# Small gaps between the tiles of a feed-forward: the same instructions at other addresses

## The chip, the cores and the metric

The kernel runs on one core of one Trainium2 chip. The metric is the time of one execution on the device, in microseconds. The engines are named TensorE (PE in the profile, PEld for its weight loads), VectorE (DVE), ScalarE (ACT), GpSimd (POOL) and SyncE (SP, which issues the DMAs here). Tiles lie in SBUF, which has 128 partitions; the address of a tile is a number of bytes within each partition. Sums of matmuls are kept in PSUM.

## What is computed

One decoder layer on a sequence of 2048 rows of 1024 numbers, in float32. The change touches the last part, the feed-forward:

```python
def reference(x, ...):
    h = rms_norm(x, g_pre_mix[l])
    proj = h @ w_in[l]
    ...                       # retention and dilated attention, joined to mix
    mix = jnp.concatenate([ret, att], axis=-1) @ w_out[l]
    x = x + rms_norm(mix, g_post_mix[l])
    h = rms_norm(x, g_pre_ffn[l])
    f = (jax.nn.silu(h @ w_gate[l]) * (h @ w_up[l])) @ w_down[l]
    x = x + rms_norm(f, g_post_ffn[l])
```

w_gate and w_up are 1024 x 2816, w_down is 2816 x 1024.

## The kernel before

The program runs five phases one after another: a norm with transposes, the input projection (L376 is its matmul), attention, the mixer with the output projection (L1034), and the feed-forward `ffn`. Each phase allocates its own tiles; when a phase ends, their room is given to the next.

**Matmuls.** Every large product is made of three: a float32 operand is split into a high part and a low part (`_hi`, `_lo`, type float32r), and hi x hi, hi x lo and lo x hi are summed in PSUM. Each matmul has a stationary tile of 128 x 128, loaded first by a weight load (LDWEIGHTS), and a moving tile of 128 x 512 that streams past it. In a call `matmul(out, a, b)` a is the stationary one and b the moving one.

**The feed-forward** takes the sequence in two halves of 1024 rows, each half as two groups (UG) of 512, and the 2816 inner columns in 11 parts (J) of 256, which are two tiles of 128. For each half, part and group:

- gate and up (L1415): for each of two tiles and for gate and up, 8 steps over the 1024 inputs, 3 products each: 24 matmuls. Stationary is a block of 128 columns of `w_hi` or `w_lo`, moving is `h_hi` or `h_lo`. The sum goes to `gu_ps`.
- ScalarE takes the silu into `gated` (L1473), VectorE multiplies by up (L1541), ScalarE copies to `a_hi` (L1475), and VectorE subtracts to `a_lo` (L1543).
- down (L1433): for each of four chunks of 128 rows and two halves of 512 output columns, 2 tiles with 3 products. Stationary is a block of `a_hi` or `a_lo`, moving is `down_hi` or `down_lo`. The sum goes to `d_ps`, and VectorE adds it to `total` (L1556, L1553).

TensorE's own order is gate_up(J, 0), down(J-1, 1), gate_up(J, 1), down(J, 0). The weights of part J+1 are loaded to `raw` and `down_raw` by SyncE while part J is computed; ScalarE makes their high parts and VectorE their low parts (L1459, L1528, L1466, L1534). At the end of each half the rows of `total` are normed (`ssq`, `squares`, `gain`), added to `x1` and stored (L1569, L1572, L1359).

**Where the tiles lie.** They are placed one after another, in the order in which they are declared, from one fixed base on; each takes a multiple of 32 bytes. Counted from that base, the tiles of the feed-forward begin at these bytes: h_hi 0, h_lo 32768, total 65536, raw 98304, w_hi 114688, w_lo 131072, down_raw 147456, down_hi 155648, down_lo 163840, gated 172032, a_hi 176128, a_lo 184320, gain 192512, x1 196608, squares 204800. All are multiples of 4096.

The input projection has hT_hi at 0 and hT_lo at 65536 (moving), `w_hi` at 135168 and `w_lo` at 143360 (stationary). The output projection of the mixer, L1034, has `w_hi` at 32768 and `w_lo` at 65536 (moving), and mT_hi at 184672 and mT_lo at 192864 (stationary). Its chain is the same three products over 8 steps:

```python
for k in range(KT):
    for a, w in ((mT_hi, w_hi), (mT_hi, w_lo), (mT_lo, w_hi)):
        last = nc.tensor.matmul(y_ps[:, half, :], a[:, s, k, :], w[:, k, half * GROUP:(half + 1) * GROUP],
```

Of the kernel before, what the change touches and what calls it, by code (L numbers as in the profile page):

```python
# [14 lines left out]
P = 128  # L15
# [1258 lines left out]
def ffn(nc, D):  # L1274
# [11 lines left out]
    with ExitStack() as ctx:  # L1286
        m = Mem(nc, ctx, "ff")
        h_hi = m.sb("h_hi", [P, KT, HALF], F32R)
        h_lo = m.sb("h_lo", [P, KT, HALF], F32R)
        total = m.sb("total", [P, UG * UC, DM])  # L1290
        raw = m.sb("raw", [P, 2, KT, PW])
        w_hi = m.sb("w_hi", [P, 2, KT, PW], F32R)
        w_lo = m.sb("w_lo", [P, 2, KT, PW], F32R)
        down_raw = m.sb("down_raw", [P, TILES, DM])
        down_hi = m.sb("down_hi", [P, TILES, DM], F32R)
        down_lo = m.sb("down_lo", [P, TILES, DM], F32R)
        gated = m.sb("gated", [P, TILES, GROUP])
        a_hi = m.sb("a_hi", [P, UG, TILES, GROUP], F32R)
        a_lo = m.sb("a_lo", [P, UG, TILES, GROUP], F32R)
        gain = m.sb("gain", [P, DM])  # L1300
        x1 = m.sb("x1", [P, 2, DM])
# [339 lines left out]
def build(nc, aps):  # L1641
    D = tensors(nc, aps)
    with ExitStack() as ctx:
        keep = {n: ctx.enter_context(nc.sbuf_tensor(n, [P, KT, SEQ], F32R)) for n in ("hT_hi", "hT_lo")}
        keep["w_raw"] = ctx.enter_context(nc.sbuf_tensor("w_raw", [P, KT, P], F32))
        spent = normed_transpose(nc, D, keep)
        project(nc, D, keep)
    with ExitStack() as ctx:
        w_out = ctx.enter_context(nc.sbuf_tensor("w_out", [P, KT, DM], F32))
        attention(nc, D, w_out, spent)  # L1650
        mix(nc, D, w_out)
    ffn(nc, D)
# [48 lines left out]
```

## Time and profile before

| | |
|---|---|
| median of the runs, us | 2872.72 (2870.31 to 2874.89) |
| profiled execution, us | 2876.43 |
| its span, first to last instruction, us | 2874.6 |
| TensorE busy | 93% of the span |
| VectorE, ScalarE, GpSimd busy | 43%, 25%, 22% |
| mean granted clock of TensorE | 0.966 |
| span moved by DMA | 269.6 MB, 94 GB/s |

TensorE's clock has two levels in the profile, 2.4 GHz (granted clock 1.00) and 1.2 GHz (0.50). The busy time that the profile gives for one matmul is longer than the distance from its start to the start of the next, since matmuls overlap. What a matmul costs in a stream of them is that distance. It is read from the starts in the timeline, or from the chain of waits, where a row gives the time that so many matmuls took together.

### The profile page before, as it was taken

Reading aid. Unit: us, or ns where it says so; the run is one execution under the profiler, and the core shown is the slowest. Engines: PE = TensorE matmul, PEld = TensorE weight load, DVE = VectorE, ACT = ScalarE, POOL = GpSimd, SP = SyncE. Lnnn points to the kernel's source line nnn. Section 1 sums busy time; section 2 is a strip of 40 time slices with the busy share of each in tenths; the row PEclk is TensorE's granted clock in tenths of the full one; section 3 lists DMA queues with packets and bytes.
Section 4 is the critical chain, followed back from the end, with each engine's and each line's share of the span. In section 5 each row is a group of like instructions: output and inputs, shape, how many; then the busy total and the mean of one; then the engine's idle time right before and its main releaser. Section 6 shows DMA issues by size and latency. Waiting matters only on the chain.

```text
span 2874.6 us, 36337 instructions
## 1 busy us (share of the span) xinstructions
PE 2663.6 (93%) x13096; PEld 2230.9 (78%) x13096; DVE 1227.9 (43%) x2271; ACT 723.0 (25%) x1402; POOL 626.8 (22%) x403
## 2 busy tenths in 40 slices
PE   6999999968989979998599999999999999999995
PEld 4777777758989857776488888888888888888884
DVE  6102455305555568886233333333354333333334
ACT  4112111116666622222111111111121111111111
POOL 2952544204443167674000000000010000000000
PEclk9999999989999979999799999999999999999998
DMA  4222223343446145654711112111253111211103
GB/s 173 70 66 66 66 102 109 117 119 106 115 123 184 50 139 170 191 169 140 263 44 45 44 44 72 45 44 44 103 179 99 44 44 44 68 49 44 44 15 102
DMA packets 220445, 269.62 MB, mean 94 GB/s; under 512 B 12224, under 2 KB 164672, under 8 KB 220096
## 3 DMA queue, kind: packets, MB, share of 16 engines
q1 hardware_dynamic: 220352, 268.42, 29.5%
q8 instruction: 53, 0.87, 0.1%
q14 instruction: 40, 0.33, 0.0%
HBM read 188.29 MB, written 80.08 MB: 93 GB/s over the span
## 4 chain that ended last, share of the span: by engine, by line
PE 49%; DMA 2%; DVE 1%; SPq 0%; issue 0%; ACT 0%; POOL 0%; DVEq 0%; ACTq 0%
PE ff_psum_gu L1415 33%; PE ff_psum_down L1433 16%; DMA out<-ff_x 1%; DMA ff_h_lo<-h_lo 0%; DMA ff_x<-x 0%; SPq L1348 0%; DVE ff_x L1572 0%; DVE ff_total L1569 0%; DVE ff_total L1556 0%; DVE ff_down_lo L1534 0%; DVE ff_w_lo L1528 0%; SPq L1353 0%; SPq L1337 0%; DVE ff_gated L1541 0%; DVE ff_total L1553 0%
## 5 line engine op out<-in xcount | busy, mean ns | idle before, releaser
L1415 PE MATMUL ff_psum_gu<-ff_h_hi,ff_w_hi 128*128 128x512 f32 x1408 | 549.6, 390 | 22.1 <-DMA ff_h_lo<-h_lo 22.1
L1415 PE MATMUL ff_psum_gu<-ff_h_lo,ff_w_hi 128*128 128x512 f32 x1408 | 549.1, 390 | 0.0
L1415 PE MATMUL ff_psum_gu<-ff_h_hi,ff_w_lo 128*128 128x512 f32 x1408 | 548.9, 390 | 0.0
L1520 POOL TENSOR_TENSOR ff_ssq<-ff_ssq,ff_minus_half 128x1 f32<-128x1 f32 x16 | 14.4, 906 | 1466.4 <-DVE ff_ssq L1561 1466.4
L1541 DVE TENSOR_TENSOR ff_gated<-ff_gated,ff_psum_gu 128x512 f32<-128x512 f32 x88 | 60.5, 687 | 628.7 <-PE ff_psum_gu L1415 628.7
L376 PE MATMUL pr_psum_acc<-hT_hi,pr_w_hi 128*128 128x512 f32 x768 | 304.1, 396 | 24.4 <-DVE pr_w_lo L315 14.2
L1415 PEld LDWEIGHTS ff_psum_gu<-ff_h_hi,ff_w_hi 128*128 128x128 f32 x1408 | 265.2, 188 | 77.9 <-issue 18.5
L1415 PEld LDWEIGHTS ff_psum_gu<-ff_h_lo,ff_w_hi 128*128 128x128 f32 x1408 | 265.3, 188 | 55.2
L1415 PEld LDWEIGHTS ff_psum_gu<-ff_h_hi,ff_w_lo 128*128 128x128 f32 x1408 | 265.1, 188 | 55.3
L376 PE MATMUL pr_psum_acc<-hT_lo,pr_w_hi 128*128 128x512 f32 x768 | 301.1, 392 | 0.0
L376 PE MATMUL pr_psum_acc<-hT_hi,pr_w_lo 128*128 128x512 f32 x768 | 301.1, 392 | 0.0
L1433 PE MATMUL ff_psum_down<-ff_down_hi,ff_a_hi 128*128 128x512 f32 x704 | 274.8, 390 | 14.9 <-DVE ff_total L1556 13.9
L1556 DVE TENSOR_TENSOR ff_total<-ff_total,ff_psum_down 128x1024 f32<-128x1024 f32 x160 | 195.2, 1221 | 202.4 <-PE ff_psum_down L1433 202.4
L1433 PE MATMUL ff_psum_down<-ff_down_hi,ff_a_lo 128*128 128x512 f32 x704 | 274.4, 390 | 0.0
L1433 PE MATMUL ff_psum_down<-ff_down_lo,ff_a_hi 128*128 128x512 f32 x704 | 274.4, 390 | 0.0
L376 PEld LDWEIGHTS pr_psum_acc<-hT_hi,pr_w_hi 128*128 128x128 f32 x768 | 145.6, 190 | 64.2 <-issue 24.4
L1475 ACT ACTIVATE ff_a_hi<-ff_gated 128x512 fp32r<-128x512 f32 x88 | 55.6, 632 | 498.9 <-DVE ff_gated L1541 498.9
L650 PE MATMUL at_psum_o<-at_vblk,at_probT 128*128 128x65 f32 x1200 | 162.8, 274 | 10.6 <-ACT at_probT L755 7.5
L1473 ACT ACTIVATE ff_gated<-ff_psum_gu 128x512 f32<-128x512 f32 x88 | 52.6, 598 | 476.0 <-PE ff_psum_gu L1415 476.0
L376 PEld LDWEIGHTS pr_psum_acc<-hT_hi,pr_w_lo 128*128 128x128 f32 x768 | 145.5, 189 | 30.9
L376 PEld LDWEIGHTS pr_psum_acc<-hT_lo,pr_w_hi 128*128 128x128 f32 x768 | 145.8, 190 | 29.7
L766 ACT ACTIVATE at_prob<-at_prob,at_orow 128x256 f32<-128x256 f32 (+1 forms) x384 | 155.2, 454 | 54.3 <-DVE at_orow L710 53.3
(158 smaller groups left out, 3979.0 us busy)
## 6 DMA issues: line engine op xcount, KB each, us to landing
ff_raw<-in_w_gate SPq DMA_DIRECT2D x22, 1024.0 KB, 5.3
ff_raw<-in_w_up SPq DMA_DIRECT2D x22, 1024.0 KB, 7.8
ff_down_raw<-in_w_down SPq DMA_DIRECT2D x22, 1024.0 KB, 4.7
projT<-pr_rows SPq DMA_DIRECT2D x64, 256.0 KB, 2.4
att_out<-at_orow SPq DMA_DIRECT2D x192, 66.0 KB, 1.8
mx_att_in<-att_out SPq DMA_DIRECT2D x16, 792.0 KB, 4.8
w_raw<-in_w_in SPq DMA_DIRECT2D x24, 512.0 KB, 4.3
nt_xin<-in_x SPq DMA_DIRECT2D x16, 512.0 KB, 3.4
```

The costliest lines, as they stand in the source:

```text
L376: last = nc.tensor.matmul(acc[:, s, g, :], w[:, s, k, :], h[:, k, t], start=n == 0, stop=n == 3 * KT - 1)
L650: last = nc.tensor.matmul(o_ps[:, j % 2, h, 0:OW], probT[:, j % 2, h, kb, :], vblk[:, j - 1 + kb, h, :], start=kb == first, stop=kb == 1)
L766: last = nc.scalar.activation(pr, pr, ACT.Exp, bias=orow[:, j % RING, 2 * OW + h:2 * OW + h + 1], scale=-1.0)
L1415: last = nc.tensor.matmul(gu_ps[:, tile, n], w[:, n, k, cols], h[:, k, t], start=i == 0, stop=i == 3 * KT - 1)
L1433: last = nc.tensor.matmul(d_ps[:, c % 2, half * GROUP:(half + 1) * GROUP], a[:, g, tile, c * P:(c + 1) * P], w[:, tile, half * GROUP:(half ...
L1473: nc.scalar.activation(gated[:, tile], gu_ps[:, tile, 0], ACT.Silu).then_inc(silu_done, 1)
L1475: nc.scalar.activation(a_hi[:, g, tile], gated[:, tile], ACT.Copy).then_inc(a_hi_done, 1)
L1520: nc.gpsimd.tensor_tensor(ssq[:, c], ssq[:, c], minus_half[:], ALU.pow).then_inc(rooted, 1)
L1541: nc.vector.tensor_tensor(gated[:, tile], gated[:, tile], gu_ps[:, tile, 1], ALU.mult).then_inc(mul_done, 1)
L1556: nc.vector.tensor_tensor(to, to, d_ps[:, c % 2], ALU.add).then_inc(added, 1)
```

## The change

Five gap tiles are declared between the tiles of the feed-forward: of 64, 64, 256, 128 and 32 bytes in each partition. Nothing reads or writes them. Every instruction is the same as before and in the same order on its engine; only the addresses in it differ. Lines behind the change are numbered 5 higher (L1415 becomes L1420, L1433 becomes L1438).

```diff
         total = m.sb("total", [P, UG * UC, DM])
         raw = m.sb("raw", [P, 2, KT, PW])
+        m.sb("gap0", [P, 16])
         w_hi = m.sb("w_hi", [P, 2, KT, PW], F32R)
+        m.sb("gap1", [P, 16])
         w_lo = m.sb("w_lo", [P, 2, KT, PW], F32R)
+        m.sb("gap2", [P, 64])
         down_raw = m.sb("down_raw", [P, TILES, DM])
         down_hi = m.sb("down_hi", [P, TILES, DM], F32R)
         down_lo = m.sb("down_lo", [P, TILES, DM], F32R)
         gated = m.sb("gated", [P, TILES, GROUP])
+        m.sb("gap3", [P, 32])
         a_hi = m.sb("a_hi", [P, UG, TILES, GROUP], F32R)
+        m.sb("gap4", [P, 8])
         a_lo = m.sb("a_lo", [P, UG, TILES, GROUP], F32R)
```

## Rows read from the trace of the kernel before

**Rows 1.** Page, part 1: engine, busy us, share of the span, instructions

```profile
PE 2663.6 (93%) x13096; PEld 2230.9 (78%) x13096; DVE 1227.9 (43%) x2271; ACT 723.0 (25%) x1402; POOL 626.8 (22%) x403
```

**Rows 2.** Timeline, TensorE, feed-forward's first matmuls: start us, us, engine, line, out<-in

```profile
1396.71 0.76 PE L1415 MATMUL ff_psum_gu<-ff_h_hi,ff_w_hi 128*128 128x512 f32 x1 [18.12 <-DMA ff_h_lo<-h_lo]
...
1397.70 0.63 PE L1415 MATMUL ff_psum_gu<-ff_h_hi,ff_w_lo 128*128 128x512 f32 x1
...
1398.98 0.63 PE L1415 MATMUL ff_psum_gu<-ff_h_hi,ff_w_lo 128*128 128x512 f32 x1
```

**Rows 3.** Timeline, all engines, the end of the program

```profile
2857.53 0.39 PE L1433 MATMUL ff_psum_down<-ff_down_hi,ff_a_lo 128*128 128x512 f32 x1
2859.24 1.22 DVE L1572 TENSOR_TENSOR ff_x<-ff_x,ff_total 128x1024 f32<-128x1024 f32 x1 [0.79 <-DMA ff_x<-x]
...
2866.72 1.28 DVE L1569 SCALAR_TENSOR_TENSOR ff_total<-ff_total,ff_ssq,ff_gain 128x1024 f32<-128x1024 f32 x1 [0.66 <-POOL ff_ssq L1520]
```

**Rows 4.** Stretches: from:to, length, busy us by engine, granted clock, DMA share, GB/s

```profile
core 0: us, PE busy (x) PEld busy (x) DVE busy (x) ACT busy (x) POOL busy (x), PEclk, DMA share, GB/s
1397.00:1399.00 2.00, 2.00 (x6) 1.52 (x6) 0.00 (x0) 0.00 (x0) 0.00 (x0) 0.50 1.11 353
1450.00:2180.00 730.00, 728.99 (x3217) 603.30 (x3216) 269.18 (x272) 128.67 (x172) 8.15 (x8) 1.00 0.21 71
```

**Rows 5.** Waits after 1400 us, TensorE's: us in total, times, longest

```profile
PE ff_psum_down L1433 <- DVE ff_total L1556: 13.9, 1, 13.9
...
PE ff_psum_gu L1415 <- DMA ff_h_lo<-h_lo: 4.0, 1, 4.0
...
PE ff_psum_down L1433 <- DVE ff_total L1553: 1.0, 1, 1.0
```

**Rows 6.** Chain of waits in order of time: start us, us, what

```profile
1491.94 21.76 PE ff_psum_gu L1415 x96
1513.70 10.88 PE ff_psum_down L1433 x48
...
2309.24 21.76 PE ff_psum_gu L1415 x96
```

**Rows 7.** Page, part 5: group, count, busy us, mean ns, idle before

```profile
L1415 PE MATMUL ff_psum_gu<-ff_h_lo,ff_w_hi 128*128 128x512 f32 x1408 | 549.1, 390 | 0.0
...
L1433 PE MATMUL ff_psum_down<-ff_down_hi,ff_a_lo 128*128 128x512 f32 x704 | 274.4, 390 | 0.0
```

**Rows 8.** Timeline, TensorE's matmuls, in the feed-forward

```profile
1499.94 0.39 PE L1415 MATMUL ff_psum_gu<-ff_h_hi,ff_w_hi 128*128 128x512 f32 x1
1500.16 0.39 PE L1415 MATMUL ff_psum_gu<-ff_h_lo,ff_w_hi 128*128 128x512 f32 x1
```

**Rows 9.** Timeline, TensorE's weight loads, the same moment

```profile
1499.94 0.19 PEld L1415 LDWEIGHTS ff_psum_gu<-ff_h_lo,ff_w_hi 128*128 128x128 f32 x1
1500.17 0.19 PEld L1415 LDWEIGHTS ff_psum_gu<-ff_h_hi,ff_w_lo 128*128 128x128 f32 x1
```

**Rows 10.** Timeline, TensorE, output projection: thirteen starts, first and last

```profile
1351.00 0.39 PE L1034 MATMUL mx_psum_y<-mx_w_hi,mx_mT_lo 128*128 128x512 f32 x1
...
1353.81 0.39 PE L1034 MATMUL mx_psum_y<-mx_w_hi,mx_mT_lo 128*128 128x512 f32 x1
```

**Rows 11.** Stretches in the output projection and early in the feed-forward, columns as above

```profile
1412.00:1416.00 4.00, 4.00 (x19) 3.34 (x18) 0.11 (x1) 0.00 (x0) 0.00 (x0) 1.00 1.05 386
1351.00:1353.90 2.90, 2.90 (x14) 2.25 (x12) 0.00 (x0) 0.00 (x0) 0.00 (x0) 1.00 0.76 231
```

**Rows 12.** Timeline, TensorE, early feed-forward: sixteen starts, first and last

```profile
1412.22 0.39 PE L1415 MATMUL ff_psum_gu<-ff_h_hi,ff_w_hi 128*128 128x512 f32 x1
...
1415.62 0.39 PE L1415 MATMUL ff_psum_gu<-ff_h_hi,ff_w_hi 128*128 128x512 f32 x1
```

**Rows 13.** Timeline, TensorE, behind a wait of the down matmuls: seven starts, then two more

```profile
2173.28 0.39 PE L1433 MATMUL ff_psum_down<-ff_down_lo,ff_a_hi 128*128 128x512 f32 x1
...
2174.67 0.39 PE L1433 MATMUL ff_psum_down<-ff_down_lo,ff_a_hi 128*128 128x512 f32 x1
2174.90 0.39 PE L1433 MATMUL ff_psum_down<-ff_down_hi,ff_a_lo 128*128 128x512 f32 x1
2175.12 0.39 PE L1433 MATMUL ff_psum_down<-ff_down_hi,ff_a_hi 128*128 128x512 f32 x1
```

## The prediction

> **What bounds the kernel now.** I read the share line of TensorE and the granted clock first, then the stretches of the feed-forward, then what TensorE waits for in it, then the chain of waits, and last the starts of single matmuls.
>
> The page says that TensorE is busy for 93% of the span, and VectorE for 43% [rows 1]. The feed-forward begins with its first matmul at 1396.71 us [rows 2] and ends with its last at 2857.53 us [rows 3]. Between 1450 and 2180 us TensorE is busy for 728.99 of 730 us at a granted clock of 1.00, which is the 2.4 GHz level, and VectorE and ScalarE are busy for 269 and 129 us [rows 4]. After 1400 us TensorE's idle time is 13.9 + 4.0 + 1.0 us, three waits in 1460 us [rows 5]. So this half of the program is one stream of matmuls, and nothing else can set its time but the distance from one matmul's start to the next.
>
> The busy time of one matmul (390 ns) is no such distance, since matmuls overlap. The chain of waits gives it: 96 gate and up matmuls take 21.76 us, 48 down matmuls take 10.88 us, both 226.7 ns each, and such rows alternate through the whole stage [rows 6]. The feed-forward has 2 x 11 x 2 x 2 x 2 x 24 = 4224 gate and up matmuls and 2 x 11 x 2 x 4 x 2 x 12 = 2112 down matmuls, 6336 in all (the page's counts are 3 x 1408 and 3 x 704 [rows 7]). 6336 x 226.7 ns = 1436 us of the 1460.8 us of the stage: **one nanosecond more or less per matmul is 6.3 us of the whole**.
>
> At the 1.2 GHz level the same matmuls start 427 ns apart: three distances from 1397.70 to 1398.98 us [rows 2]. The granted clock there is 0.50 [rows 4]. That is 512 columns at 1.2 GHz (426.7 ns) with nothing on top. At 2.4 GHz the columns alone would be 213.3 ns, but the rows show 226.7. So 13.3 ns of each matmul, 84 us of the program, is something that the slow clock hides, and the only other thing that TensorE does at that moment is to read the next stationary tile: while the matmul of 1499.94 us runs, the load for the next one starts, at 1499.94 us too, and takes 0.19 us [rows 8, 9].
>
> **Does an address matter at all?** The change alters nothing but base addresses, so I looked for two places in this trace that do the same thing at different ones. Write every base as a distance in bytes from the first tile of its phase. In the feed-forward before, all bases are multiples of 4096. The input projection's tiles (hT_hi 0, hT_lo 65536, w_hi 135168, w_lo 143360) are multiples of 4096 too. The output projection of the mixer (L1034) has its moving tiles at multiples of 4096, but its stationary tiles mT_hi and mT_lo at 184672 and 192864, 352 bytes past one. 352 is an odd multiple of 32, every other distance is a multiple of 64.
>
> Its matmuls have the same shape and type, and the same order of three products as the down matmuls. Yet twelve distances from 1351.00 to 1353.81 us take 2.81 us, **234.2 ns each and not 226.7** [rows 10]. Other engines are not the reason: in that stretch VectorE, ScalarE and GpSimd are busy for 0.00 us, at a granted clock of 1.00 [rows 11]. The DMA engines are not either: they are at 0.76 there, while between 1412 and 1416 us they are at 1.05 [rows 11] and fifteen gate and up distances from 1412.22 to 1415.62 us are 226.7 ns each all the same [rows 12]. What is left as the difference is the address of the stationary tile: 7.5 ns a matmul.
>
> A third thing shows in the feed-forward itself: after a wait the distance is not 226.7 at once. From 2173.28 us the next six distances are 1.39 us together, **231.7 ns each**, before it settles at 226.7 or so (2174.67, 2174.90, 2175.12) [rows 13]. So 226.7 is a rhythm that the matmuls fall into, and while anything keeps disturbing it the mean is some 5 ns higher.
>
> **The change, part by part.** No instruction is added, removed or reordered; the gap tiles are never touched. Bases after, as distances from h_hi: w_hi 114752 (+64), w_lo 131200 (+128), down_raw, down_hi, down_lo and gated +384, a_hi +512, a_lo +544, gain, x1 and squares +544. h_hi, h_lo, total and raw stay, as does everything before the feed-forward: 0 us there.
>
> - Gate and up, 4224 matmuls: moving h stays, the stationary tiles shift by 64 and 128 bytes and remain multiples of 64. No row shows such a shift alone. Bounds: 0, or what the mixer's address shows, 7.5 x 4224 = +31.7 us; below nothing, the whole excess, -13.3 x 4224 = -56.2 us. The strides within w_hi and w_lo give the nearest evidence: column blocks 512 bytes apart run at one distance, so shifts of 512 and its multiples do nothing. Whether 64 and 128 do is not shown; I take **0**, since the one slow place differs by an odd multiple of 32, which these shifts are not.
> - Down, 2112 matmuls: moving down_hi and down_lo shift by 384, the stationary a_hi by 512 (nothing by the above), a_lo by 544, an odd multiple of 32 like mT's 352. One weight load in three, 704, gets the mixer's kind of address. Low: only these pay, 704 x 7.5 = +5.3 us. High: the rhythm is lost for all three products, 2112 x 7.5 = +15.8 us. Between them is the case that one disturbed load in three never lets it settle, the price of [rows 13]: 2112 x 5.0 = **+10.6 us**. I take this, as the settling takes six matmuls and the disturbance returns every third.
> - VectorE and ScalarE operands, and the weight transfers: hidden, because VectorE is busy for 269 of 730 us and TensorE waits for no transfer there. If an operation took twice its time they would still fit.
> - The end: from 2857.53 us the last rows of the output go through gain, x1 and squares, shifted by 544, 17.1 us with no cover. Its VectorE operations are 1.2 to 1.3 us each [rows 3]. I take 0, at most 1 us either way.
>
> Sum: 0 + 10.6 + 0 + 0 = +10.6 us. The profiled execution's own time is 2876.4 us with a span of 2874.6; it lies 3.7 us above the median of 2872.7. Against its own time the changed kernel would be 2887; against the median, which I forecast, **2872.7 + 10.6 = 2883.3 us**, and 2878 to 2889 by the two bounds of the down term.
>
> The rows show each load under the matmul before it [rows 8, 9]. The Trainium skill, in TensorE: Matmul & The Clock Gate, Step-by-step, says that loading the next tile's weights "doesn't steal SBUF read bandwidth from the running matmul", and SBUF — State Buffer, under the two separate sides, that PE never waits on anyone. By that rule no address could matter, and the time would be that before; the 234.2 beside 226.7 ns speaks against it, but does not prove the address. The first of these pages also gives 215.7 ns for 512 columns back to back; the rows show 226.7, so whatever the 11 ns between them are, it is a cost that some arrangement may not have.
>
> **The rivals.**
> - *No difference.* The mixer's pace has another cause (its PSUM tile, the operations around it), or a_lo's shift costs under 2 ns a load. For it: the feed-forward keeps one distance for three pairs of tiles with bases tens of kilobytes apart. Against it: beyond its address and its PSUM tile nothing in [rows 10] differs from the down matmuls. That the gaps don't move the tiles at all belongs here; since sizes are whole multiples of 32 bytes they do. Time: 2872.7, within 3.
> - *Slower all over.* What counts is that moving and stationary bases are congruent modulo 128 or more, which before holds for every fast place and after for none. Its place is the gate and up stage as well: it decides as soon as the shift of 64 costs over 1.4 ns. Gate and up alone, 2872.7 + 31.7 = 2904; with down, 6336 x 7.5 = +47.5, 2920 us.
> - *Faster.* Both streams start on the same multiple, so that each weight read meets the matmul's reads in the same part of the memory; moving one by 64 bytes takes it out of the way. Its ceiling is 13.3 x 6336 = 84 us, 2788 us; half of it 2830. For it: the excess is there, and absent at the slow clock. Against it: a weight load sweeps 512 bytes while the matmul sweeps 2048, so a shift under 512 moves where they meet, not how often; and no settled distance under 226.7 stands anywhere in the trace.
>
> **How the numbers follow.** Forecast 0.35, no difference 0.25, slower all over 0.21, faster 0.19. The likeliest gives 2883. Its low end is about the 0.2% (5.7 us) that a measurement can tell from no change, so 0.03 of it counts as same: faster 0.19, same 0.28, slower 0.53. The range must take in no difference and slower all over (2920), and may leave out most of faster: 2862 to 2922, which leaves out about 0.18 below and 0.02 above; signs are mixed, and the forecast's own range stands above.
>
> **What would show it.** In the profile after, the chain's rows for 48 down matmuls would read 11.0 to 11.3 instead of 10.88, and those for 96 gate and up matmuls 21.76. Gate and up rows at 22.1 or more mean slower all over; 21.5 or less, faster. The mixer must be unchanged. A down row of 10.88 makes the reading of the mixer wrong; a time that moved with both rows unchanged makes all of it wrong.

## The result: 1.2% slower

| | before | changed |
|---|---|---|
| median, us | 2873.46 (2870.31 to 2874.89) | 2909.22 (2905.06 to 2910.40) |
| ratio, 95% interval | | 1.0123 (1.0106 to 1.0141) |
| profiled span, us | 2874.6 | 2908.6 |
| granted clock, mean | 0.966 | 0.963 |

The changed kernel takes 35.8 us more, where +10.6 was forecast. In the profile after, the chain of waits in order of time (start us, us, what) reads:

```profile
1517.97 11.20 PE ff_psum_down L1438 x48
1529.17 22.19 PE ff_psum_gu L1420 x96
...
2331.26 22.19 PE ff_psum_gu L1420 x96
2353.44 11.20 PE ff_psum_down L1438 x48
```

These answer to [rows 6]. 96 gate and up matmuls take 22.19 us instead of 21.76, which is 231.1 ns from start to start instead of 226.7. 48 down matmuls take 11.20 us instead of 10.88, 233.3 ns each. There are 44 blocks of each kind, so the rows give 44 x 0.43 + 44 x 0.32 = 18.9 + 14.1 = **33.0 us** of a span that grew by 34.0 us.

Nothing else moved. These are the waits of TensorE after 1400 us (us in total, times, longest):

```profile
PE ff_psum_gu L1420 <- DMA ff_h_lo<-h_lo: 21.1, 2, 18.3
PE ff_psum_down L1438 <- DVE ff_total L1561: 13.8, 1, 13.8
PE ff_psum_down L1438 <- DVE ff_total L1558: 0.5, 1, 0.5
```

And this is the stretch of [rows 4] again, with its columns:

```profile
core 0: us, PE busy (x) PEld busy (x) DVE busy (x) ACT busy (x) POOL busy (x), PEclk, DMA share, GB/s
1450.00:2180.00 730.00, 730.00 (x3151) 591.44 (x3150) 256.83 (x259) 123.92 (x166) 8.14 (x8) 1.00 0.20 67
```

The first row holds the feed-forward's first wait of 18.3 us, which in the kernel before (18.12 us) ended just ahead of 1400 us [rows 2]; without it 2.8 us are left where [rows 5] has 4.0. So the idle time is that of before, the clock is 1.00 as before, and VectorE and ScalarE do the same work at a slower rate. TensorE has 3151 matmuls in 730 us, where it had 3217. The same instructions each start later. Starts of single matmuls, fifteen distances apart:

```profile
1599.93 0.40 PE L1420 MATMUL ff_psum_gu<-ff_h_hi,ff_w_hi 128*128 128x512 f32 x1
...
1603.40 0.40 PE L1420 MATMUL ff_psum_gu<-ff_h_hi,ff_w_hi 128*128 128x512 f32 x1
```

3.47 us / 15 = 231.3 ns, against the 226.7 of [rows 12].

### The profile page after: what moved, and what is told of

The parts are those of the page before. It is cut to its first block, busy times and chain, and to the rows that moved or that the text cites. A ratio compares the mean times of both kernels' runs of the same rounds, so it can differ in the third digit from the quotient of the medians.

```text
span 2908.6 us, 36337 instructions
## 1 busy us (share of the span) xinstructions
PE 2692.2 (93%) x13096; PEld 2228.2 (77%) x13096; DVE 1228.9 (42%) x2271; ACT 722.7 (25%) x1402; POOL 630.4 (22%) x403
## 4 chain that ended last, share of the span: by engine, by line
PE 49%; DMA 2%; DVE 1%; SPq 0%; issue 0%; ACT 0%; POOL 0%; DVEq 0%; ACTq 0%
PE ff_psum_gu L1420 33%; PE ff_psum_down L1438 17%; DMA out<-ff_x 1%; DMA ff_x<-x 0%; DMA ff_h_lo<-h_lo 0%; SPq L1353 0%; DVE ff_x L1577 0%; DVE ff_total L1561 0%; DVE ff_total L1574 0%; DVE ff_down_lo L1539 0%; DVE ff_w_lo L1533 0%; POOL ff_ssq L1525 0%; SPq L1342 0%; DVE ff_gated L1546 0%; DVE ff_total L1558 0%
## 5 line engine op out<-in xcount | busy, mean ns | idle before, releaser
L1420 PE MATMUL ff_psum_gu<-ff_h_hi,ff_w_hi 128*128 128x512 f32 x1408 | 561.9, 399 | 21.1 <-DMA ff_h_lo<-h_lo 21.1
L1420 PE MATMUL ff_psum_gu<-ff_h_hi,ff_w_lo 128*128 128x512 f32 x1408 | 553.7, 393 | 0.0
L1420 PE MATMUL ff_psum_gu<-ff_h_lo,ff_w_hi 128*128 128x512 f32 x1408 | 550.8, 391 | 0.0
L1420 PEld LDWEIGHTS ff_psum_gu<-ff_h_hi,ff_w_hi 128*128 128x128 f32 x1408 | 265.3, 188 | 79.7 <-issue 18.6
L1420 PEld LDWEIGHTS ff_psum_gu<-ff_h_hi,ff_w_lo 128*128 128x128 f32 x1408 | 265.6, 189 | 67.3
L1420 PEld LDWEIGHTS ff_psum_gu<-ff_h_lo,ff_w_hi 128*128 128x128 f32 x1408 | 265.7, 189 | 58.7
L1438 PE MATMUL ff_psum_down<-ff_down_hi,ff_a_hi 128*128 128x512 f32 x704 | 277.4, 394 | 14.3 <-DVE ff_total L1561 13.8
L1438 PE MATMUL ff_psum_down<-ff_down_lo,ff_a_hi 128*128 128x512 f32 x704 | 281.5, 400 | 0.0
L1438 PE MATMUL ff_psum_down<-ff_down_hi,ff_a_lo 128*128 128x512 f32 x704 | 278.5, 396 | 0.0
L1438 PEld LDWEIGHTS ff_psum_down<-ff_down_hi,ff_a_hi 128*128 128x128 f32 x704 | 132.8, 189 | 49.1 <-DVE ff_total L1561 14.2
```

The source lines that it names most:

```text
L1420: last = nc.tensor.matmul(gu_ps[:, tile, n], w[:, n, k, cols], h[:, k, t], start=i == 0, stop=i == 3 * KT - 1)
L1438: last = nc.tensor.matmul(d_ps[:, c % 2, half * GROUP:(half + 1) * GROUP], a[:, g, tile, c * P:(c + 1) * P], w[:, tile, half * GROUP:(half ...
```

## The experiments

### Only the shifts of gate and up

```diff
         raw = m.sb("raw", [P, 2, KT, PW])
+        m.sb("gap0", [P, 16])
         w_hi = m.sb("w_hi", [P, 2, KT, PW], F32R)
+        m.sb("gap1", [P, 16])
         w_lo = m.sb("w_lo", [P, 2, KT, PW], F32R)
+        m.sb("gap2", [P, 96])
         down_raw = m.sb("down_raw", [P, TILES, DM])
```

> Only the stationary tiles of gate and up are shifted as in the change (w_hi +64, w_lo +128 bytes against h); down's tiles are shifted by 512 together. Theory A (the distance from matmul to matmul is set by where its own stationary and moving tiles lie, modulo 512): 96 gate and up matmuls take 22.19 us as in the changed kernel, 48 down matmuls 10.88 us as before; 4224 x 4.5 ns = +19 us over before. Rival B (the slower pace comes from the addresses that VectorE, ScalarE or the transfers use, or from the down tiles): gate and up stay at 21.76 us and the time at +0. Rival C (large shifts like 512 matter too): down leaves 10.88.

Measured: 2893.82 against 2873.77 us, ratio 1.0066 (1.0051 to 1.0082), +20.0 us. The first matmuls of one gate and up block, of the down block behind it, and of the next block, in the timeline of TensorE:

```profile
1722.63 0.40 PE L1418 MATMUL ff_psum_gu<-ff_h_hi,ff_w_hi 128*128 128x512 f32 x1
...
1744.82 0.39 PE L1436 MATMUL ff_psum_down<-ff_down_hi,ff_a_hi 128*128 128x512 f32 x1
...
1755.70 0.40 PE L1418 MATMUL ff_psum_gu<-ff_h_hi,ff_w_hi 128*128 128x512 f32 x1
```

22.19 us for the 96, as in the changed kernel, and 10.88 us for the 48, as before. Theory A holds, but for its period, which this run leaves open: shifts of 64 and 128 bytes are enough, and down, whose tiles all lie 512 bytes further, is untouched. B and C fall as they are put. VectorE and ScalarE also write `w_hi` and `w_lo` at the shifted addresses here; that their writes are not what costs is shown only by the scan below, where no other engine works.

### Only the shifts of down

```diff
         w_lo = m.sb("w_lo", [P, 2, KT, PW], F32R)
+        m.sb("gap2", [P, 96])
         down_raw = m.sb("down_raw", [P, TILES, DM])
@@
+        m.sb("gap3", [P, 32])
         a_hi = m.sb("a_hi", [P, UG, TILES, GROUP], F32R)
+        m.sb("gap4", [P, 8])
         a_lo = m.sb("a_lo", [P, UG, TILES, GROUP], F32R)
```

> Only down_raw, down_hi, down_lo, gated (+384), a_hi (+512) and a_lo (+544) are shifted as in the change; gate and up lie as before. Theory A: gate and up 21.76 us for 96, down 11.20 us for 48 as in the changed kernel; 2112 x 6.7 ns = +14 us. Rival B: down stays at 10.88 us because the weights of gate and up disturb the whole stream.

Measured: 2885.61 us, ratio 1.0038 (1.0025 to 1.0051), +11.8 us. The chain of waits:

```profile
1514.94 11.19 PE ff_psum_down L1436 x48
1526.13 21.79 PE ff_psum_gu L1418 x96
```

Down runs as in the changed kernel, so B falls. Gate and up take 21.79 us, 0.03 more than before: in the trace the first five distances of a block are 228.4 to 235.8 ns in the mean of the blocks, and from the sixth on they are 226.7, much as in [rows 13]. The two halves, 20.0 and 11.8 us, make 31.8 of the 35.8; the rest is within the intervals of the three measurements. For this part the blocks give 44 x 0.31 + 44 x 0.03 = 15.0 us, and the runs 7 to 15, so the runs say less than the blocks of what down costs.

### The mixer's stationary tiles aligned

```diff
+        m.sb("gap0", [P, 40])
         mT_hi = m.sb("mT_hi", [P, 2, KT, P], F32R)
         mT_lo = m.sb("mT_lo", [P, 2, KT, P], F32R)
```

> Before, with one gap of 160 bytes ahead of mT_hi in the mixer, so that mT_hi and mT_lo lie at a multiple of 512 bytes from the moving tiles instead of 352 past a multiple of 4096. Theory A: the output projection's distance falls from 234.2 to 226.7 ns; 768 matmuls x 7.5 ns = 5.8 us at most, less where the mixer waits for VectorE: -2 to -5.8 us. Rival (the output projection is slower for its PSUM tile or its surroundings): 234.2 ns and the time stay.

Measured: 2872.85 us, ratio 0.9995 (0.9986 to 1.0004). The output projection (L1034 is L1035 here), twelve distances apart in the timeline:

```profile
1347.01 0.39 PE L1035 MATMUL mx_psum_y<-mx_w_hi,mx_mT_hi 128*128 128x512 f32 x1
...
1349.73 0.39 PE L1035 MATMUL mx_psum_y<-mx_w_hi,mx_mT_hi 128*128 128x512 f32 x1
```

2.72 us / 12 = 226.7 ns, where [rows 10] had 234.2 with the same PSUM tile and surroundings. So the reading of [rows 10] was right: it was the address. But little of the 5.8 us reaches the time: its interval is -4.0 to +1.1 us, which holds nothing as well as the upper part of the expected -2 to -5.8. The stretch from the first to the last matmul of the output projection says why. First the kernel before, with the columns as above:

```profile
1050.10:1368.70 318.60, 296.10 (x1474) 234.06 (x1474) 243.45 (x486) 89.27 (x178) 189.28 (x167) 0.99 0.52 163
```

Then the kernel with the gap:

```profile
1047.30:1364.70 317.40, 291.15 (x1474) 233.45 (x1474) 242.63 (x485) 89.41 (x178) 189.33 (x167) 0.99 0.54 163
```

For the same 1474 matmuls TensorE is busy 5.0 us less, but the stretch is only 1.2 us shorter. The rest turns into waits; the two longest in the kernel with the gap are for VectorE.

```profile
PE mx_psum_tp L953 <- DVE mx_hT_lo L1163: 13.2, 12, 1.2
PE mx_psum_y L1035 <- DVE w_out L1067: 11.4, 14, 2.5
```

The first of them was 9.5 us before, the second 11.4 too. The 1.2 us are from one trace of each kernel, but the other six kernels of this case that leave the mixer alone take 318.3 to 318.8 us there as well, so about a fifth of the 5.8 us seems to be kept. In the mixer TensorE waits for VectorE again and again; in the feed-forward it does not, and every nanosecond of a matmul counts.

### A scan of shifts

The chains of this program, and the tuple of shifts in bytes that each chain takes (stationary hi, stationary lo, moving hi, moving lo):

```python
for c, (sh, sl, mh, ml) in enumerate(SETS):
    for i in range(N):
        k, q = (i // 3) % 8, i % 3
        st, so = (stat_hi, sh) if q < 2 else (stat_lo, sl)
        mv, mo = (mov_hi, mh) if q != 1 else (mov_lo, ml)
        a = k * 128 + so // 4
        b = k * 512 + mo // 4
        last = nc.tensor.matmul(ps[:, c % 4], st[:, a:a + 128], mv[:, b:b + 512],
                                start=i == 0, stop=i == N - 1)
```

> None of the layer is computed: 62 chains of 48 matmuls of 128 x 512 in float32r, each chain with its own shift of the stationary and moving tiles, no other engine at work during them. Theory A: 226.7 ns at no shift, 231.1 for the changed kernel's gate and up shifts (64 and 128), 233.3 for its down shifts (128 and 160 against 384), about 234 for a stationary shift of 352; equal shifts of both tiles give 226.7 if only their difference counts. If a conflict in the memory is avoidable by an address, some shift gives under 226.7, down to 213.3 to 216. Rival B: 226.7 in every chain.

Of each chain the last 24 distances were averaged, from the starts in the timeline. Here are the two ends of that stretch for no shift, for the stationary tiles at +96, for all four tiles at +96, for the changed kernel's down, which is (0, 32, 384, 384) up to multiples of 512, and for (128, 160, 384, 384). In the last one the high stationary tile is 256 bytes from the moving tiles, and only the low one is off, by 32 modulo 256; the text on record ahead of the run takes it for the changed kernel's down, which it is not.

```profile
29.90 0.39 PE L61 MATMUL ps<-mov_hi,stat_lo 128*128 128x512 f32 x1
...
35.34 0.39 PE L61 MATMUL ps<-mov_hi,stat_lo 128*128 128x512 f32 x1
...
118.85 0.40 PE L61 MATMUL ps<-mov_hi,stat_lo 128*128 128x512 f32 x1
...
124.47 0.39 PE L61 MATMUL ps<-mov_hi,stat_lo 128*128 128x512 f32 x1
...
507.51 0.39 PE L61 MATMUL ps<-mov_hi,stat_lo 128*128 128x512 f32 x1
...
512.95 0.40 PE L61 MATMUL ps<-mov_hi,stat_lo 128*128 128x512 f32 x1
...
595.13 0.39 PE L61 MATMUL ps<-mov_hi,stat_lo 128*128 128x512 f32 x1
...
600.73 0.39 PE L61 MATMUL ps<-mov_hi,stat_lo 128*128 128x512 f32 x1
...
673.15 0.39 PE L61 MATMUL ps<-mov_hi,stat_lo 128*128 128x512 f32 x1
...
678.75 0.39 PE L61 MATMUL ps<-mov_hi,stat_lo 128*128 128x512 f32 x1
```

5.44, 5.62, 5.44, 5.60 and 5.60 us for 24. The means of the chains with one shift, in ns:

| shift in bytes | 0 | 32 | 64 | 96 | 128 | 160 | 192 | 224 | 256 |
|---|---|---|---|---|---|---|---|---|---|
| stationary only | 226.7 | 233.3 | 233.3 | 234.4 | 232.8 | 233.3 | 228.9 | 233.3 | 226.7 |
| the same + 256 | 226.7 | 233.3 | 233.3 | 234.4 | 232.7 | 233.3 | 228.9 | 233.3 | 226.7 |
| moving only | 226.7 | 233.3 | 228.9 | 233.3 | 233.3 | | 233.3 | | 226.7 |
| both | 226.7 | 226.7 | 226.7 | 226.7 | 226.7 | | 226.7 | | 226.7 |

- The pattern repeats with 256 bytes, and at multiples of 32 bytes it is the difference of the two bases that counts. Moving the moving tile by 64 is the same as moving the stationary one by 192, and the other way round. Half a period, 128, does not settle at one value: 232.8 and 232.7 with the stationary tiles, 233.3 with the moving ones, and of two chains with the moving tiles at +384 one has 233.3 and one 232.0.
- Among the shifts tried, only a difference of 0 modulo 256 gives 226.7. The changed kernel's gate and up (64, 128, 0, 0) gives 231.1 and its down 233.3, exactly what its rows show. The mixer's 352 is 96 modulo 256, and gives 234.4 (234.2 in the layer).
- One tile of the four is enough. The low stationary tile alone at +32 slows the whole chain to 233.3, as much as both stationary tiles do; either stationary tile alone at +64 gives 231.1.
- Below 32 bytes moving both tiles together is not safe: both at +16 231.1 ns, both at +4 237.8 ns.
- The lowest of all 62 chains is 226.7. No shift that was tried gains.

### The table carried back to the layer

Three kernels, each the kernel before with gaps of other sizes. The first has 256 bytes in all five gaps:

> The five gaps of the change at the same places, each of 256 bytes instead of 64, 64, 256, 128 and 32. If only the difference of the two bases modulo 256 counts: 21.76 and 10.88 us as before, and no difference in time (within 3 us). If gaps or moved tiles as such cost something: 5 to 36 us more.

Measured: 2872.88 us against 2874.69 for the kernel before, run beside it, ratio 0.9999 (0.9987 to 1.0010). The second has one gap, `m.sb("gap0", [P, 24])`, ahead of h_hi:

> One gap of 96 bytes ahead of the first tile of the feed-forward, so that all its tiles move together and none lies at the old place modulo 256. If only the difference counts: as before, within 3 us. If each tile's own address counts: 96 gate and up matmuls take 22.1 us or more, and the time is 20 to 50 us over before.

Measured: 2874.10 us against the same 2874.69, ratio 0.9994 (0.9981 to 1.0007). Their chains, in that order:

```profile
1519.90 21.76 PE ff_psum_gu L1420 x96
1541.66 10.88 PE ff_psum_down L1438 x48
```

```profile
1524.83 21.76 PE ff_psum_gu L1416 x96
1546.59 10.88 PE ff_psum_down L1434 x48
```

Both are the kernel before to the hundredth, with every tile behind the gaps at another address. The third puts the stationary tiles alone at +96:

```diff
+        m.sb("gap0", [P, 24])
         w_hi = m.sb("w_hi", [P, 2, KT, PW], F32R)
         w_lo = m.sb("w_lo", [P, 2, KT, PW], F32R)
+        m.sb("gap1", [P, 40])
         down_raw = m.sb("down_raw", [P, TILES, DM])
@@
+        m.sb("gap2", [P, 24])
         a_hi = m.sb("a_hi", [P, UG, TILES, GROUP], F32R)
```

> Stationary tiles alone at +96 bytes modulo 256 (w_hi, w_lo, a_hi, a_lo), moving ones at 0: the worst shift of the scan, 234.4 ns. Sum by the scan: 6336 x 7.75 ns = +49 us, 22.50 us for 96 gate and up and 11.25 us for 48 down matmuls, worse than the change. If the scan of bare chains doesn't carry over: anything else.

Measured: 2920.11 us against the same 2874.69, ratio 1.0157 (1.0140 to 1.0174), +45.4 us, and in the timeline 22.49 us for the 96 and 11.25 for the 48:

```profile
1726.19 0.40 PE L1418 MATMUL ff_psum_gu<-ff_h_hi,ff_w_hi 128*128 128x512 f32 x1
...
1748.68 0.39 PE L1436 MATMUL ff_psum_down<-ff_down_hi,ff_a_hi 128*128 128x512 f32 x1
...
1759.93 0.39 PE L1418 MATMUL ff_psum_gu<-ff_h_hi,ff_w_hi 128*128 128x512 f32 x1
```

22.50 and 11.25 were expected from the scan, which so carries over to the layer within a hundredth of a microsecond a block. The sum of 49 us lies in the interval of the ratio, 40 to 50 us.

### What the excess is: two scans that leave it open

> None of the layer is computed: 39 chains of 48 matmuls with other numbers of stationary columns (128, 96, 64, 32), of moving columns (512, 384, 256) and in bfloat16. If the 13.3 ns over the columns' time, and what a shift adds, are the stream held up by the reads of the next weight load: the excess falls with the stationary columns (13.3, 10, 7, 3 ns at no shift), stays the same with fewer moving columns, and in bfloat16, with half the bytes, it is 2 to 3 ns and the shift does nothing. If the excess is a fixed cost of each matmul: 13.3 ns whatever the stationary columns, and in bfloat16 too.

Measured, ns from start to start, mean of the last 24 (groups of another number format or size follow the same code, with the numbers of columns in the slices):

| stationary x moving columns | columns alone | no shift | +32 | +96 | +192 |
|---|---|---|---|---|---|
| 128 x 512 | 213.3 | 226.7 | 233.3 | 234.5 | 228.9 |
| 96 x 512 | 213.3 | 230.0 | 228.9 | 233.3 | 233.3 |
| 64 x 512 | 213.3 | 230.0 | 231.7 | 226.7 | 228.3 |
| 32 x 512 | 213.3 | 231.7 | 240.0 | 230.5 | 231.7 |
| 128 x 384 | 160.0 | 173.3 | | 173.3 | |
| 128 x 256 | 106.7 | 120.0 | | 117.3 | |
| 128 x 512, bfloat16 | 213.3 | 215.8 | 215.8 | 215.8 | 215.8 |

The expected fall from 13.3 to 3 ns with fewer stationary columns is not there: the chain with 32 columns has 24 distances in 5.56 us.

```profile
168.11 0.40 PE L65 MATMUL ps<-mov_hi,stat_lo 128*32 128x512 f32 x1
...
173.67 0.40 PE L65 MATMUL ps<-mov_hi,stat_lo 128*32 128x512 f32 x1
```

So the excess does not shrink with the next load's columns, as that reading asks, though the load itself does: its records take 190, 161, 134 and 108 ns for 128, 96, 64 and 32 columns. The reading's two other marks are there: with 384 and 256 moving columns the excess at no shift is 13.3 ns again, and in bfloat16 it is 2.5 ns and no shift does anything. The rival, a fixed cost of each matmul, falls by bfloat16. The program also runs eight shifts of the first scan once more, in 128 x 512 float32r, and each mean is within 0.1 ns of that in the scan of shifts. The stretch with only bfloat16 chains shows 223 weight loads in 48 us, 215.2 ns each (columns: length, TensorE's matmuls, its weight loads, ScalarE, GpSimd, granted clock, DMA share, GB/s; three records of matmuls are missing):

```profile
236.00:284.00 48.00, 47.79 (x220) 21.72 (x223) 0.00 (x0) 0.00 (x0) 1.00 0.00 1
```

The Trainium skill, in TensorE: Matmul & The Clock Gate, "Wait — 56ns, not 53.3ns?", gives 215.7 ns for 512 columns back to back. In bfloat16 these chains agree (215.8); in float32r they do not, at any address tried.

> None of the layer is computed: 35 chains of 48 matmuls in float32r. Question 1, which two tiles have to agree modulo 256: a matmul's moving tile with its own stationary tile, or with the stationary tile of the next matmul, whose load runs meanwhile. Chains in which both bases alternate between 0 and d (own difference 0, difference to the next d), and chains in which own difference is d and that to the next 0. If the load that runs meanwhile counts: the second kind gives 226.7 ns, the first over 228. If a matmul's own pair counts: the other way round. Question 2: with 384 moving columns the shift of 96 did nothing; if the shift only matters where the stream leaves no time over, 416 to 496 columns show where it begins, and each excess is 13.3 ns or more.

Measured, with d alternating on one or both tiles:

| d | own difference 0, to the next d | own difference d, to the next 0 |
|---|---|---|
| 32 | 233.4 | 233.3 |
| 64 | 231.7 | 233.3 |
| 96 | 234.3 | 230.0 |
| 128 | 236.7 | 230.0 |

Neither kind gives 226.7, so the question as put has no answer: agreement with the own stationary tile alone is not enough, nor is agreement with the next one alone. In these chains each tile also differs in base from the one before it, and no chain separates that. One chain, own difference 128, to the next 0, is perfectly even at 230.0 ns (24 distances in 5.52 us):

```profile
118.45 0.39 PE L61 MATMUL ps<-mov_hi,stat_lo 128*128 128x512 f32 x1
...
123.97 0.39 PE L61 MATMUL ps<-mov_hi,stat_lo 128*128 128x512 f32 x1
```

For question 2: 384 moving columns are at 173.3 for shifts of 0, 32 and 192 and between 174.5 and 176.7 for the others. The shift of 96 takes 176.7 here and took 173.3 in the scan before, with the tiles at the same places, so a shift does not always settle at the same distance. 416, 448 and 480 columns take 186.7, 206.7 and 216.7 ns at no shift and at 96 alike, 496 take 223.3 and 226.7. The excesses run from 13.3 to 20 ns with no order by size. Two chains that read the same blocks in every matmul give 226.7 at no shift and 234.4 at 96, so the steps from block to block are not the cause. **The cause of the excess, and why the difference modulo 256 decides, stays open.** What is shown is at which shifts the distance is lowest, and that in bfloat16, the one other type tried, no shift matters.

## Why the prediction was right or wrong, point by point

- **TensorE's distance from start to start as the only thing that counts: right.** Waits and clock stayed as they were, and 33.0 of 34.0 us of span are that distance times its count.
- **An address matters at all: right.** The mixer with its tiles aligned falls from 234.2 to 226.7 ns. The Trainium skill's sentence that loading the next tile's weights "doesn't steal SBUF read bandwidth from the running matmul" (TensorE: Matmul & The Clock Gate, Step-by-step), as the prediction reads it, would have made the time equal. With float32r at the 2.4 GHz level the difference between the bases of the stationary and the moving tile decides (226.7 against 234.4 ns), so reading the one is not independent of reading the other, and the runs decide. Whether what is lost is bandwidth, they do not show.
- **Gate and up, 0 us: wrong, the step that failed.** It measured +18.9 us by the chain and +20.0 by the run of this part alone. The step took one slow place, 352 bytes off, and read it by its lowest bit, an odd multiple of 32. It is 96 modulo 256, and every other multiple of 32 that the scan tried is slow too, unless it is a multiple of 256 (231.1 ns for the shifts of this step). The row that was right beside it, blocks 512 bytes apart at one distance, only bounded the period from above; the text said so, and then chose 0. Its own bounds, 0 to +31.7, held.
- **Down, +10.6 us: the direction and the bounds right, the size short, and one shift counted as free that is not.** It measured +14.1 by the chain (+11.8 by the run of this part alone), within 5.3 and 15.8. The mechanism was half right. That one load in three slows all three products is what the scan shows for a low stationary tile alone at +32; but it is a stable slower rhythm of three, 6.7 ns each, and not a settling that starts anew every third matmul (5.0 ns each). And a_lo is not the only cause: the moving tiles' 384 bytes were taken for nothing, and put a_hi 128 bytes off as well; alone they give 232.0 and 233.3 ns in the scan.
- **The other operands, the transfers and the end, 0 us: right, as far as it can be told.** From the last matmul to the end it is 17.1 us before and 2908.6 - 2892.75 = 15.9 after, and 15.7 to 17.1 in all eight profiles of the layer:

```profile
2892.75 0.39 PE L1438 MATMUL ff_psum_down<-ff_down_hi,ff_a_lo 128*128 128x512 f32 x1
```

- **The rivals, and the range.** The range held (2909 in 2862 to 2922) because it took in "slower all over"; the forecast, 2883, missed by 26 us. "Slower all over" is what happened, in its mechanism (congruence of the two bases modulo 128 or more; the scan says 256) and its place. Its price of 47.5 us took the mixer's 7.5 ns for all matmuls; the kernel with all stationary tiles at +96 shows that price (+45.4), and the change's own shifts cost 4.5 and 6.7 ns. "Faster" has no shift to stand on: no mean of a 128 x 512 float32r chain is under 226.7.

## What to carry to other kernels

Where TensorE is the bound and runs float32r with 512 moving columns, keep the bases of all stationary and moving tiles congruent modulo 256 bytes and multiples of 32. Tiles of whole multiples of 256 bytes do it, and one small tile declared between them undoes it: in these chains that cost 1 to 3% of the matmuls' time. This was seen with 128 stationary and 512 moving columns; with fewer stationary columns another shift is the best of those tried (64 columns: 226.7 at +96, 230.0 at 0). To see it in a profile, divide a row of the chain of waits by its count: the busy time of a matmul, 390 ns before and 391 to 400 after, doesn't give it. And before taking a gain of this kind from a table of matmuls, look at what TensorE waits for in that stage: in the mixer the same 7.5 ns, 5.8 us by their count, shortened the stretch by 1.2 us and the time by nothing that the runs can tell.

## What the runs showed of the hardware that was not expected

- A chain of float32r matmuls of 128 x 512 falls into a rhythm that depends on the bases, and keeps it: 226.7 ns at a difference of 0 modulo 256, 228.9 to 234.4 at other multiples of 32, up to 238.0 with the moving tiles at +4. One tile out of line is enough (233.3 with the low stationary tile alone at +32).
- A stream that leaves a slower rhythm carries it for some matmuls into a well aligned one (21.79 instead of 21.76 us for 96).
- Fewer columns don't shorten a matmul in proportion. At no shift 32 stationary columns make it slower (231.7 against 226.7 ns), and 480 moving columns take 216.7 ns where the columns alone are 200.0.
- The lowest distance is not always that of no shift: 256 moving columns take 120.0 and 120.1 ns there, and 117.3 and 118.8 at +96.
